# A statistics tile 56 columns narrower, and everything allocated behind it 224 bytes further down

## The reference

```python
for layer in range(DEPTH):
    z = rmsnorm(x, norm_mix[layer]) @ w_in[layer]            # 1024 x 2964
    ...
    x = x + jnp.concatenate([o_a, o_b, o_c, o_d], axis=-1) @ w_out[layer]
    h = rmsnorm(x, norm_ffn[layer])
    x = x + (jax.nn.silu(h @ w_gate[layer]) * (h @ w_up[layer])) @ w_down[layer]
```

```python
x = x + rms_norm(h, norm_g[i, 1])
h = squared_relu_mlp(rms_norm(x, norm_g[i, 2]), mlp_w1[i], mlp_w2[i])
x = x + rms_norm(h, norm_g[i, 3])
```

## Time and profile before

| | |
|---|---|
| median of 3 runs | 1992.79 us |
| lowest and highest | 1992.78 and 1993.23 us |
| the profiled execution | 1993.23 us |
| its span, first to last instruction | 1991.4 us |
| TensorE busy (matmuls) | 1971.4 us, 99% |
| VectorE busy | 1342.5 us, 67% |
| ScalarE busy | 965.2 us, 48% |
| transfers | 351.68 MB, 177 GB/s over the span |

### The profile page before, as it was taken

How to read it: one execution, slowest core, us unless ns; L and a number is a source line. 1 busy time by engine, 2 the same in 40 slices (tenths; PEclk the granted TensorE clock), 3 DMA queues, 4 the chain that set the end, 5 groups by cost and what they waited for, 6 DMA issues and landing times.

```text
span 1991.4 us, 26383 instructions
## 1 busy us (share of the span) xinstructions
PE 1971.4 (99%) x11046; PEld 1670.7 (84%) x11046; DVE 1342.5 (67%) x1496; ACT 965.2 (48%) x1148; POOL 46.3 (2%) x89
## 2 busy tenths in 40 slices
PE   8999999999999999999999999999999999999998
PEld 6889888888988887788888688888888888778887
DVE  5876666687566775676568865566865667667565
ACT  6655444755544543354445554454544444345443
POOL 0000000000000000000000000000000000000000
PEclk9999999999999999999999999999999999999999
DMA  7425654523665555545657355547565555455653
GB/s 243 141 83 173 198 188 164 171 96 123 220 198 186 189 170 190 169 148 192 207 193 210 124 198 187 189 152 230 193 202 187 173 193 188 157 173 172 197 189 106
DMA packets 239558, 351.68 MB, mean 177 GB/s; under 512 B 15952, under 2 KB 134096, under 8 KB 239440
## 3 DMA queue, kind: packets, MB, share of 16 engines
q1 hardware_dynamic: 238864, 349.27, 53.8%
q10 hardware_dynamic: 576, 0.73, 0.1%
HBM read 344.83 MB, written 1.05 MB: 174 GB/s over the span
## 4 chain that ended last, share of the span: by engine, by line
PE 95%; DVE 1%; ACT 1%; DMA 1%; issue 0%; SPq 0%; DVEq 0%; ACTq 0%
PE psD L2199 20%; PE psD L2212 15%; PE psD L2213 15%; PE psD L2217 13%; PE psD L2203 9%; PE psD L2181 3%; PE psD L2180 3%; PE psD L2185 3%; PE psD L2215 2%; PE psD L2531 1%; DMA raw<-in_w_in 1%; PE psD L2479 1%; PE psD L2603 1%; PE psD L2604 1%; PE psD L2844 1%; PE psD L2296 1%
## 5 line engine op out<-in xcount | busy, mean ns | idle before, releaser
L1211 DVE TENSOR_TENSOR wl<-raw,wh 128x2048 fp32r<-128x2048 f32 (+2 forms) x327 | 723.5, 2219 | 258.1 <-ACT wh L675 257.4
L675 ACT ACTIVATE wh<-raw 128x2048 fp32r<-128x2048 f32 (+2 forms) x327 | 605.2, 1854 | 306.3 <-PE psD L2215 243.0
L2199 PE MATMUL psD<-AHL,wh 128*128 128x512 f32 x1664 | 589.2, 398 | 0.0
L2203 PE MATMUL psD<-AHL,wl 128*128 128x256 f32 x1560 | 438.1, 281 | 0.0
L2199 PEld LDWEIGHTS psD<-AHL,wh 128*128 128x128 f32 x1664 | 312.7, 188 | 77.5
L2212 PE MATMUL psD<-wh,HH 128*128 128x512 f32 x864 | 339.5, 393 | 0.1
L2213 PE MATMUL psD<-wl,HH 128*128 128x512 f32 x864 | 336.5, 389 | 0.0
L2203 PEld LDWEIGHTS psD<-AHL,wl 128*128 128x128 f32 x1560 | 294.6, 189 | 1.2
L2217 PE MATMUL psD<-wh,HL 128*128 128x512 f32 x735 | 286.6, 390 | 0.0
L2212 PE MATMUL psD<-wh,AHL 128*128 128x512 f32 (+3 forms) x516 | 199.3, 386 | 2.5 <-DVE AHL L1247 1.7
L2213 PE MATMUL psD<-wl,AHL 128*128 128x512 f32 (+3 forms) x516 | 192.8, 374 | 0.0
(11 more groups left out here) (403 smaller groups left out, 2252.0 us busy)
## 6 DMA issues: line engine op xcount, KB each, us to landing
raw<-in_mlp_w SPq DMA_DIRECT2D x128, 1024.0 KB, 5.4
raw<-in_ret_w_in SPq DMA_DIRECT2D x48, 1024.0 KB, 5.1
raw<-in_w_gate SPq DMA_DIRECT2D x20, 1024.0 KB, 5.3
raw<-in_w_up SPq DMA_DIRECT2D x20, 1024.0 KB, 5.3
raw<-in_w_down SPq DMA_DIRECT2D x20, 1024.0 KB, 5.2
raw<-in_ret_w_out SPq DMA_DIRECT2D x16, 1024.0 KB, 5.1
raw<-in_w_in SPq DMA_DIRECT2D x15, 1024.0 KB, 5.3
raw<-in_cf_w_pw SPq DMA_DIRECT2D x12, 1024.0 KB, 6.4
```

Of the source, the lines that this page charges most:

```text
L675: e.activation(wh[q % NHL][:, 0:kt * n], raw[q % NRAW][:, 0:kt * n], ACT.Copy).then_inc(*up("act_wh", q))
L1211: e.tensor_tensor(wl[q % NHL][:, 0:kt * n], raw[q % NRAW][:, 0:kt * n], wh[q % NHL][:, 0:kt * n].bitcast(F32), ALU.subtract).then_inc(*up( ...
L2199: e.matmul(o, hi[:, k, fs], both[:, k, :, :], start=k == 0, stop=False, skip_group_check=True)
L2203: e.matmul(o[:, S:2 * S], lo[:, k, fs], AH[:, k, :], start=False, stop=k == 7, skip_group_check=True)
```

## The change

The tile `ST` gets 888 columns in place of 944. Everything allocated behind it (`HH0` to `GFC`) starts 224 bytes lower in each partition, `HH0` at 135584 in place of 135808 and `AR` at 151968 in place of 152192. Instructions, waits, shapes and transfers are the same.

```diff
--- before.py
+++ after.py
@@ -283,7 +283,7 @@
         ONES = sb("ONES", [P, P])
         MH = sb("MH", [P, 8])
         s4 = XS[:, 0, :].rearrange("p (a n) -> p a n", a=4)
-        ST = sb("ST", [P, 944])
+        ST = sb("ST", [P, 888])
         HH = [sb(f"HH{i}", [P, 4, S], FR) for i in range(2)]
         HL = [sb(f"HL{i}", [P, 4, S], FR) for i in range(2)]
         AR = sb("AR", [P, 16384])
```

## The result

The changed kernel takes 2005.33 us at the median of 5 runs (2004.96 to 2006.32), the one before 1992.79 us in 5 runs on the same chip (1992.32 to 1993.34). The ratio is 1.0066, with a 95% interval of 1.0055 to 1.0077. The forecast was 1992.8 us, no change, in a range of 1991.0 to 1995.0; the time lies 10.3 us above that range.

The account below looks back on a forecast made before the run. TensorE was taken as the bound, its matmuls in flight for 1971.4 of 1991.4 us. Four terms of 0 against the profiled execution's 1993.23 us, 0.44 us above the three runs' median, gave 1992.8 us, range 1991.0 to 1995.0.

Parts of the forecast that it names:

- no change: Whole kernel: time differs by under 0.2%, or 4.0 us, from before; chance 0.88.
- Weight loads from moved tensors: TensorE's 2832 matmuls with `HH` or `HL` stationary: any longer load stays hidden, 0 us; without cover 2.8 us.
- Operands that stream: TensorE's 1518 matmuls that touch `AR` or `EX`: 0 us, with 1.5 us to either side for the range.
- VectorE and ScalarE: Their work on the moved `HH`, `HL`, `AR` and `EX`: 0 us, at 0.6% longer or shorter 0.24 us.
- Transfers: Transfers into or out of moved tensors, chiefly convolution tap copies: 0 us, with 0.6 us left before TensorE would wait.
- The sum against the profiled execution: Whole kernel: four terms of 0 against the profiled execution's 1993.23 us; forecast for the median 1992.8 us.
- (a): Rival, loads from `HH` and `HL` 32 bytes off a 64 byte boundary not hidden: slower, 1998.5 us at 2 ns; chance 0.07.
- (b): Rival, large tensors' common start modulo 4096 ends for 2832 matmuls: faster, 1987.1 us at 2 ns, 1956 at most; chance 0.05.
- The forecast's last sentence: Named what would make it wrong: a place cost that neither duration nor start shows in the compared rows; no size.

Follow-up runs that it names:

- e1_st896: `ST` cut to 896 columns from the 944 of the kernel before the change, everything behind it 192 bytes lower: 1999.53 us, ratio 1.0035.
- e6_all_32: 8 unused columns ahead of `raw` in the kernel before the change, everything 32 bytes higher, all distances kept: 1992.55 us, ratio 0.9998.
- e8_ahl32: Kernel before the change with 8 unused columns in front of `AHL` and 56 behind it: 1984.80 us, ratio 0.9961.

## Why the prediction was wrong, point by point

**Weight loads from moved tensors: 0.** This is the step that failed. It argued that a load from `HH` lasts 188 ns, one from `MK`, 32 bytes off, 186 to 189, and that 38 ns of each step cover the rest: "So the place of the stationary operand is worth at most 1 or 2 ns, and 38 ns cover them". The term measures 14.7 us (14.8 with `HH` and `HL` moved alone), 5.2 ns for each of 2832. Three things in it were wrong. The duration of the load is not where the cost is: it stays 188 ns while the step goes from 227.2 to 233.3. The 38 ns are no cover against it, since the step grows with the load as long as before. And `MK` was no control: its matmuls stream from `MK` itself, at multiples of 512 bytes from the stationary 128 columns, so that the two operands are 0 apart modulo 256. The question had been put as one of place, and the load's duration was compared where the step is what costs.

**Operands that stream: 0, within 1.5 us.** Right for what moved: with `AR`, `EX` and `GFC` moved alone the time is 1992.66 us. But the reasons were weak. The rows with `ONES` are fp32, and the fp32 form doesn't feel a distance (430.3 ns at all three). The tiles of 396 columns of `wl` were compared by duration, and at a length where the step behaves otherwise (for 384 columns 174.7, 174.6 and 177.8 ns at 0, 32 and 64 bytes). Neither could have shown what the 512 column form loses.

**VectorE and ScalarE: 0.** Right: 1343.0 and 965.3 us after, 1342.5 and 965.2 before, the write into `HL` takes 1226 ns for 1225, and no wait of a matmul changed by more than 0.3 us.

**Transfers: 0.** Right: the taps land after 3.4 us at the median as before, and moving `AR` alone costs nothing. The estimate of 0.02 us a transfer that I worked out by the Trainium skill, "DMA: Bandwidth & Descriptors", section "How a descriptor splits into AXI transactions", can't be told from zero in that median.

**The sum against the profiled execution.** It stood on the right base. The effect of 13.5 us of span is just the one missing term, 14.7 - 1.0 = 13.7 us, the 1.0 being the column products, which no step had.

**The rivals.** (a) had the sign, the place ("in the MLPs and not where `AHL` is stationary") and the threshold right: 5.2 ns is over its 1.4 ns. Its price went by the `MK` rows, 2 ns and 1998.5 us, and its cause, the 64 byte boundary, is refuted by e1_st896 and e6_all_32. (b) looked at what mattered, that all large tensors stand alike, and got the sign wrong for this form: for the 512 column row products the common start is the good case. For the column products it is indeed the bad one, and the 7.7 us of e8_ahl32 are what leaving it gave there, net of what `AHL` lost where it is stationary. The forecast's last sentence named the case, a cost "that needs two moved operands at once", though one moved operand and one unmoved were enough, and gave it no chance of its own. A chance of 0.88 for no change was far too much for an effect that no row before could show, with 2832 tight steps exposed to it: 1.4 ns in 227 was enough to leave the band.

## What to carry to other kernels

When a tensor moves in the on-chip memory, ask for each tight fp32r matmul form how far its stationary operand is from its streamed one, modulo 256 bytes, and measure steps from start to start: an unchanged load duration says nothing. A control must have the same form, type and length and differ in the very relation that the change alters. In a kernel that is all matmuls, padding of 32 bytes is worth a sweep: here a shift of 32 bytes modulo 256 cost 12.5 us at one place and gave 7.7 us at another. The gain has to be measured and not only worked out, since the column products also change with what stands around them.

## What the runs showed of the hardware that was not expected

- A row product in fp32r with 512 streamed columns has a step of 228.1 ns when stationary and streamed operand are 0 apart modulo 256 bytes, 229.5 to 230.2 ns at a few offsets (stationary +192 and +240) and 232 to 238 ns at the others, with no other engine at work. Which part of the memory or of TensorE the load and the stream share was not shown; that they share one is inferred from the period of 256 bytes. Nor is it shown whether a load meets the stream of its own matmul or that of the one before: in every row product here both stand at the same offset.
- The effect has another sign at 256 columns (120.9 ns at 0, 114.6 at 64 bytes), is nothing at 128 (112.2 ns at 0, 32 and 64), and an fp32 matmul of 512 columns is free of it (430.3 ns at all three).
- Column products, 512 columns and 256 by turns, have two levels at the same addresses, about 177 and 174 ns a step without the slow first one. Straight behind row products the level followed these: 177.2 ns at 0, 174.0 at +32, 177.3 at +64. With their streamed operand 32 bytes off they were at the low one in all groups. Why is open, and so is why the kernel shows the reverse: its column products won 1.0 us beside row products at +32 and 8.3 us beside ones at +64.
